# Router logits of six tiles with the router's weights stationary, in four column groups

## What is computed

```
x = x + mixed @ w_out[l]
...
h = rms_norm(x, norm_ffn_g[l])            # (1024, 1024)
logits = (h @ router_w + router_b)        # (1024, 32)
top_val, top_idx = lax.top_k(logits, 4)
gates = jax.nn.softmax(top_val, axis=-1)
```

## Time and profile before

| | us |
|---|---|
| median of 3 runs | 2224.8 (2224.79 to 2225.76) |
| the profiled execution, its own time | 2226.86 |
| its span, first to last instruction | 2225.1 |
| TensorE busy in it | 2172.1 (98%) |
| VectorE busy | 1385.5 (62%) |
| ScalarE busy | 564.5 (25%) |
| GpSimd busy | 251.9 (11%) |
| the 128 records of line 894 (all eight tiles), TensorE | 15.2 |

### The profile page before, as it was taken

One profiled execution on the slowest core, in us unless ns is written; L12 is line 12 of the kernel. 1 busy time (PEld: TensorE's weight loads), 2 busy tenths in 40 slices (PEclk: granted clock), 3 DMA queues, 4 the chain that ended last, 5 costly groups with the idle time before them and its releaser, 6 DMA issues.

```text
span 2225.1 us, 39664 instructions
## 1 busy us (share of the span) xinstructions
PE 2172.1 (98%) x14677; PEld 1876.5 (84%) x14679; DVE 1385.5 (62%) x2836; ACT 564.5 (25%) x1239; POOL 251.9 (11%) x231
## 2 busy tenths in 40 slices
PE   8999999999999999999999999999999999999996
PEld 4444454556679999999999999989999999999996
DVE  3352232577657778776877678755655666667565
ACT  2122221344412222222222222211211222222113
POOL 1000000022140010101010101000000000010003
PEclk9999999999999999999999999999999999999998
DMA  8000002211158999898999899966977788799778
GB/s 314 37 38 1 0 1 75 77 55 58 49 197 284 311 315 306 287 303 298 309 300 324 273 304 312 317 201 223 303 251 230 231 290 270 249 303 302 228 247 302
DMA packets 244083, 488.26 MB, mean 219 GB/s; under 512 B 24135, under 2 KB 24343, under 8 KB 243876
## 3 DMA queue, kind: packets, MB, share of 16 engines
q1 hardware_dynamic: 223684, 452.48, 58.9%
q0 software_dynamic: 20128, 35.01, 6.8%
q10 hardware_dynamic: 224, 0.16, 0.0%
HBM read 476.59 MB, written 48.58 MB: 236 GB/s over the span
## 4 chain that ended last, share of the span: by engine, by line
PE 95%; DVE 2%; issue 1%; DMA 1%; ACT 1%; SPq 0%; POOL 0%; DVEq 0%; POOLq 0%
PE PS L1019 69%; PE PS L688 15%; PE PS L875 5%; PE PS L848 1%; PE PS L815 1%; PE PS L837 1%; DMA pairB<-acc_dram 1%; PE PS L894 0%; DVE unit L1574 0%; PE PS L661 0%; PE PS L760 0%; PE PS L683 0%; ACT unit L1267 0%; DMA pairB<-in_x_dram 0%; PE PS L981 0%
## 5 line engine op out<-in xcount | busy, mean ns | idle before, releaser
L1019 PE MATMUL PS<-pairA,unit 128*128 x12288 | 1541.1, 289 | 15.6 <-issue 14.3
L1019 PEld LDWEIGHTS PS<-pairA,unit 128*128 128x128 f32 x12288 | 1536.4, 191 | 20.5 <-issue 19.1
L1785 DVE STREAM_TRANSPOSE unit<-unit 32x512 f32<-32x512 f32 x496 | 315.2, 636 | 7.9 <-DMA unit<-h_dram,cur_x 1.1
L1804 DVE STREAM_TRANSPOSE pairA<-unit 32x512 f32<-32x512 f32 x496 | 315.2, 636 | 6.9
L688 PE MATMUL PS<-pairA,unit 128*128 128x512 f32 (+1 forms) x528 | 231.1, 594 | 1.4 <-issue 1.4
L1313 ACT ACTIVATE unit<-PS,cur_b 128x256 f32<-128x256 f32 x256 | 107.3, 471 | 395.2 <-PE PS L1019 331.9
L1296 ACT ACTIVATE unit<-unit 128x512 f32<-128x512 f32 x128 | 80.5, 630 | 471.6 <-DVE unit L1829 471.5
L688 PEld LDWEIGHTS PS<-pairA,unit 128*128 128x128 f32 (+1 forms) x528 | 97.4, 188 | 116.3 <-issue 115.5
L1302 ACT ACTIVATE unit<-PS,cur_b 128x256 f32<-128x256 f32 x256 | 107.3, 471 | 306.0 <-PE PS L1019 306.0
L596 POOL DMA_INDIRECT acc_dram<-pairA,cur_y x62 | 99.5, 1605 | 699.2 <-ACT pairA L1286 689.0
L1840 DVE TENSOR_SCALAR unit<-unit 128x512 f32<-128x512 f32 x128 | 54.6, 427 | 160.8 <-ACT unit L1302 157.6
(11 more groups left out here) (254 smaller groups left out, 1124.8 us busy)
## 6 DMA issues: line engine op xcount, KB each, us to landing
unit<-in_expert_w_gu_dram SPq DMA_DIRECT2D x256, 1024.0 KB, 5.3
unit<-in_expert_w_down_dram SPq DMA_DIRECT2D x128, 1024.0 KB, 7.7
unit<-in_w_in_dram SPq DMA_DIRECT2D x6, 2048.0 KB, 15.8
pairB<-in_x_dram SPq DMA_DIRECT2D x16, 512.0 KB, 13.0
unit<-in_w_out_dram SPq DMA_DIRECT2D x2, 2048.0 KB, 8.8
h_dram<-pairA SPq DMA_DIRECT2D x8, 512.0 KB, 2.6
acc_dram<-pairB SPq DMA_DIRECT2D x8, 512.0 KB
pairB<-acc_dram SPq DMA_DIRECT2D x8, 512.0 KB, 11.9
```

What stands on the lines that cost most here:

```text
L1019: ins = pe.matmul(ps[:, ITEM * (j % 2):ITEM * (j % 2) + w], slot_w[s][:, k, P * j:P * j + P], xa_cols[:, ITEM * kd:ITEM * kd + KD * ITEM + ...
L1785: ins = dve.transpose(cols[:, :, :, 32 * q:32 * q + 32], rows[:, :, :, 32 * a:32 * a + 32])
L1804: ins = dve.transpose(rows[:, :, :, 32 * a:32 * a + 32], cols[:, :, :, 32 * q:32 * q + 32])
```

## The change

For tiles 0 to 5 route(t) exchanges the operands. The router's block rw[:, k, :] (128 x 32) is stationary and the tokens' block of h2T moves (128 columns). The result is transposed, 32 experts x 128 tokens, and stands in 32 of PSUM's 128 partitions. Four such products go to the four groups of 32 columns of the array: block k = 2q + j goes to group q, two blocks accumulate in each. That leaves four partial sums, stacked in the partitions. ScalarE copies the 128 x 128 stack to logit_parts (take_parts, the memory of no_rows used anew), between its copies of the weights and the exponentials of step u = 4t + 11. One product with logit_parts stationary and fold moving (fold is four identity matrices of 32 stacked, made by GpSimd at the start) sums the four parts and turns them back: sum_logits(t), one step later, directly ahead of out_project(t+1, 0). It writes to another part of the same bank, where choose(t) reads. Tiles 6 and 7 stay as they were. Two transfers of the bias table are counted on the semaphore small_in instead of one of their own, and the unused wide_ps goes.

```diff
+        logit_parts, fold = no_rows[:, 0:P].bitcast(F32), sb("fold", [P, N_EXP])
...
-        N_SMALL = 6 + 4
+        N_SMALL = 6 + 4 + 2
...
+            step.do(pool.memset(fold[:, :], 0.0))
+            for q in range(4):
+                ins = pool.affine_select(out=fold[:, :], in_=fold[:, :], compare_op=ALU.not_equal, fill=1.0, base=-32 * q,
+                                         pattern=[[-1, N_EXP]], channel_multiplier=1)
...
-            pe.wait_ge(table_in, 32)
...
-                for k in range(KD):
-                    ins = pe.matmul(ps[:, 0:N_EXP], h2T[t % 2][:, k, :], rw[:, k, :], start=(k == 0), stop=(k == KD - 1))
-                ins.then_inc(logits_done, 1)
+                if t >= NT - 2:
+                    for k in range(KD):
+                        ins = pe.matmul(ps[:, 0:N_EXP], h2T[t % 2][:, k, :], rw[:, k, :], start=(k == 0), stop=(k == KD - 1))
+                    ins.then_inc(logits_done, 1)
+                    return
+                for j in range(2):
+                    for q in range(4):
+                        ins = pe.matmul(ps[32 * q:32 * q + 32, 0:P], rw[:, 2 * q + j, :], h2T[t % 2][:, 2 * q + j, :],
+                                        start=(j == 0), stop=(j == 1))
+                ins.then_inc(parts_done, 1)
+
+            def sum_logits(t):
+
+                if t == 0:
+                    pe.wait_ge(consts, 6)
+                pe.wait_ge(parts_ready, t + 1)
+                pe.matmul(bank(ring_bank["logits", t])[:, P:P + N_EXP], logit_parts, fold[:, :],
+                          start=True, stop=True).then_inc(logits_done, 1)
...
                 if u % 4 == 0 and t >= 0:
+                    if t >= 1:
+                        sum_logits(t - 1)
                     out_project(t, 0)
...
-            act.dma_start(table[:, :], rel_bias_table).then_inc(table_in, 16)
-            act.dma_start(one_hot, buckets).then_inc(table_in, 16)
+            act.dma_start(table[:, :], rel_bias_table).then_inc(small_in, 16)
+            act.dma_start(one_hot, buckets).then_inc(small_in, 16)
...
+            def take_parts(t):
+                if t == 0:
+                    act.wait_ge(list_clear, 32)
+                else:
+                    act.wait_ge(logits_done, t)
+                act.wait_ge(parts_done, t + 1)
+                act.activation(logit_parts, bank(ring_bank["logits", t])[:, 0:P], ACT.Copy).then_inc(parts_ready, 1)
...
+                if u % 4 == 3 and u >= 11:
+                    take_parts((u - 11) // 4)
                 if u < len(da_units):
                     da_exps(u)
...
-                dve.scalar_tensor_tensor(out=lg[:, :], in0=bank(ring_bank["logits", t])[:, 0:N_EXP], scalar=rstd[:, t:t + 1],
+                lo = P if t < NT - 2 else 0
+                dve.scalar_tensor_tensor(out=lg[:, :], in0=bank(ring_bank["logits", t])[:, lo:lo + N_EXP], scalar=rstd[:, t:t + 1],
                                          in1=rb_wide[:, :], op0=ALU.mult, op1=ALU.add).then_inc(logits_read, 1)
```

More of the change, by code:

```diff
@@ L247, in build @@
          rstd_ready, x_scaled, x_turned, hT_ready, proj_done, proj_evac, conv_done, sig_done, qk_done,
-         log_f_part, em_in, em_ready, cols_ps, cols_ready, wide_ps, wide_ready,
+         log_f_part, em_in, em_ready, cols_ps, cols_ready, wide_ready,
          dve_step, act_step, pool_step) = (sem(n) for n in (
@@ L252, in build @@
              "proj_evac", "conv_done", "sig_done", "qk_done", "log_f_part", "em_in", "em_ready",
-             "cols_ps", "cols_ready", "wide_ps", "wide_ready", "dve_step", "act_step",
+             "cols_ps", "cols_ready", "wide_ready", "dve_step", "act_step",
              "pool_step"))
@@ L287, in build @@
             "gate_bias_clear", "pool_waited", "y_sent", "strip_spread"))
-        ident_ready, table_in, gate_w_in, lam_in_sem, router_in, squared, gain_rows_in, ml_divided, \
+        ident_ready, gate_w_in, lam_in_sem, router_in, squared, gain_rows_in, ml_divided, \
             ml_squared, da_squared, sum_squared = (sem(n) for n in (
-            "ident_ready", "table_in", "gate_w_in", "lambda_in", "router_in", "squared",
+            "ident_ready", "gate_w_in", "lambda_in", "router_in", "squared",
             "gain_rows_in", "ml_divided", "ml_squared", "da_squared",
@@ L295, in build @@
         out_sent, wide_out = sem("out_sent"), sem("wide_out")
+        parts_done, parts_ready = sem("parts_done"), sem("parts_ready")
         spot_ready, last_summed = sem("spot_ready"), sem("last_summed")
@@ L515, in _ @@
                                pattern=[[1, P]], channel_multiplier=-1).then_inc(consts, 1)
+            step.do(pool.memset(fold[:, :], 0.0))
+            for q in range(4):
+                ins = pool.affine_select(out=fold[:, :], in_=fold[:, :], compare_op=ALU.not_equal, fill=1.0, base=-32 * q,
+                                         pattern=[[-1, N_EXP]], channel_multiplier=1)
+                if q < 3:
+                    step.do(ins)
+            ins.then_inc(consts, 1)
             for n in range(NT):
```

## The result

| | before | changed |
|---|---|---|
| median of 22 runs each, us | 2225.07 (2224.06 to 2227.45) | 2229.74 (2227.85 to 2231.96) |
| ratio to before | | 1.0018, 95% interval 1.0013 to 1.0024 |
| profiled execution: own time, span | 2226.86, 2225.1 | 2230.08, 2228.2 |

What follows compares the result with a forecast made beforehand. TensorE, busy 98% of the span, was taken as the bound. Tile 0 +0.69, tile 1 +0.73, tiles 2 to 4 +0.09, tile 5 +0.73 made 2.24 us more: median 2227.1 us, range 2223.2 to 2231.0.

Steps and rivals of the forecast that it cites:

- The hand-over: Ahead of each out_project TensorE sums, VectorE reads the logits, only then TensorE goes on: costs 0.73 us a tile.
- The limit by da_max: da_logit behind route(t) waits for VectorE's maximum; usable saving 0.70 us in tiles 2 to 4, 0.04 in tile 0.
- The grouped product: route(t) in four column groups side by side: 0.43 us plus 0.31 for the edges, 0.74 us, 0.97 less than before.
- VectorE's shift in tile 4: VectorE's read of the logits moves 2.27 us later into 2.36 us of idle time, so it just fits.
- The expert loop: Rival: the 3.20 us TensorE stall ahead of the loop changes by up to 3 us either way; chance 0.14.
- Together 2.24 us more: Sum over tiles 0 to 5 of hand-over cost less usable saving, carried through to the end of the kernel.
- The first case: The main forecast, saving and hand-over as priced: +0.9 to +3.8 us; chance 0.52.
- the groups that do not run side by side: Rival: route(t) takes 2.02 us, 0.31 more than before; sum 6.0 us, 2230.8 us; chance 0.17.

Runs made afterwards that it cites:

- e5: Changed kernel with useless products in TensorE's gaps, including eight ahead of the last transposes of step 32; 2228.41 us, ratio 1.0012 to the kernel before.
- e2: Kernel before, plain product kept, only its eighth and last part moved directly ahead of out_project; 2229.71 us, ratio 1.002.
- e1: Changed kernel with sum_logits(t) moved earlier, to the end of the step of route(t), behind da_values; 2223.4 us, ratio 0.9988 to the kernel before.

## Why the prediction was right, and where it fell short

- **The hand-over.** Forecast 0.73 us a tile; measured 0.80 to 0.83 in tiles 1 and 5, where nothing stands against it, and 0.68 in tile 0 once its gaps are filled (e5), net of what da_logit gains there. The waits stand where they were said to: six times VectorE on the sum, six times TensorE on the read, 0.43 us each. In tile 4 the read ends at 562.10 + 0.25 = 562.35 and TensorE starts at 562.49, 0.14 us later, where I had 0.06 from da_logit, and the eight records behind it take 3.67 us, 0.07 more than 3.60 and not 0.10. e2 shows that the hand-over costs this time without the grouped form.
- **The limit by da_max.** Forecast: 0.70 us usable in tiles 2 to 4, 0.04 in tile 0, nothing elsewhere. Without the hand-over, in e1, 0.72 to 0.80 us are gained in tiles 2 to 4 and 0.13 in tile 0. I had added 0.10 us for weights not loaded ahead, and read it wrongly: the 3.70 us of the earlier trace rows follow da_logit with no wait between, and behind its new wait da_logit takes 1.13 us in tile 0 and 1.99 in tile 4, as before. That saving and hand-over cancel to 0.02 us in tiles 2 to 4, as forecast, is in part luck: both were some 0.1 us larger than forecast.
- **The grouped product.** Forecast 0.74 us, measured 0.58. If the four rounds take 0.107 us each, the edges cost some 0.15 and not 0.31 us; the rows do not part the two. Little hung on it, since the limit by da_max lets through no more than 0.8 us of the saving.
- **VectorE's shift in tile 4.** Forecast 0.1 us to spare; 0.19 us are left. ScalarE's copies cost nothing: it starts them 0.1 to 0.2 us after the product and ends them ahead of the maximum.
- **The expert loop.** The stall ahead of it was 3.20 us before, 3.38 and 3.25 in the two profiles of the changed kernel, and between 3.05 and 3.62 us over all eight. So that rival has a share of 0.2 us at most in the changed kernel, and not the 3 us that it allowed for.
- **The step that was missing.** "Together 2.24 us more" is the term that was too small: the sum has no clock in it. I had worked out that TensorE would stand still ahead of da_logit in tiles 0 and 1 and ahead of every output projection, and priced the waits only by their length. In tile 0 the granted clock fell behind two of these waits, and the four records behind them paid another 1.7 us. With it the structural 2.35 become 4.03 us in the loop; the medians are 4.67 us apart, and the last 0.6 us are not traced.
- **The range.** The first case, the one that came true, had its own range from +0.9 to +3.8 us. The medians are 4.67 us apart, above it. That the time still lies in the whole range is luck: it reached so far up for the groups that do not run side by side, and they do.

## What to carry to other kernels

A product whose result another engine must read before TensorE may go on belongs well ahead of that point; directly ahead of it, it costs a round trip (0.8 us here), whatever the product itself saves. Look for the wait that becomes the last one when a product is shortened, and then for what the new gap does to the clock. Four column groups with 32 columns each are worth having where the time that they free can be used: here 0.58 us instead of 1.87 in one group, and instead of 1.71 in the plain form.

## What was not expected of the hardware

In tile 0 of the changed kernel, in both profiles, a gap of 0.78 us and one of 0.43 us, 1.5 us apart, were followed by four records at 1.2 GHz: 0.85 us each instead of 0.43. In tiles 1 and 5 of the same profiles longer gaps were not. With products of no use in the gaps the clock stayed at 1.00 through the loop (e5), and the kernel was faster than without them (2228.41 against 2230.14 us). Four groups of float32 products with 32 stationary and 128 moving columns ran 16 records in 0.58 us, 0.036 us a record, where one group had 0.117.
